# The opening layer as one program: recurrent and stick-breaking heads in 41 steps between the projections and the output product

## What is computed

```python
hn = rmsnorm(h, mix_norm[0])
qa, ka, va, qb, fb, ib, gb = split(hn @ w_in)          # seven parts of 512 columns
# stick-breaking: 8 heads of 64
z = (qa @ ka.T) / 8
log_keep = where(s < t, log_sigmoid(-z), 0)
w = where(s < t, exp(log_sigmoid(z) + later_sum(log_keep)), 0)
o_a = w @ va
# recurrent (HGRN2): 4 heads of 128, state carried from chunk to chunk
log_f = log(lb + (1 - lb) * sigmoid(fb));  k = (1 - lb) * sigmoid(-fb);  q = silu(qb)
b = cumsum(log_f)
o_b = (q exp(b)) @ state + causal(sum_k q k exp(b_t - b_s)) @ ib
o_b = rmsnorm(o_b, hg_norm) * silu(gb)
h = h + concat(o_a, o_b) @ w_out
```

## Time and profile before

| | |
|---|---|
| three runs | 3671.11, 3674.70, 3677.27 us; median 3674.7 |
| profiled execution | 3672.74 us, span 3670.9 us, mean granted clock 0.976 |
| PE busy | 3476.9 us (95%), 16522 matmuls |
| DVE, ACT, POOL busy | 1706.3 us (46%), 924.6 us (25%), 2172.9 us (59%) |
| opening layer | from 0 to 490.9 us |

### The profile page before, as it was taken

How to read it: one execution, slowest core, us unless ns; L and a number is a source line. 1 busy time by engine, 2 the same in 40 slices (tenths; PEclk the granted TensorE clock), 3 DMA queues, 4 the chain that set the end, 5 groups by cost and what they waited for, 6 DMA issues and landing times. The chain is left out here.

```text
span 3670.9 us, 46256 instructions
## 1 busy us (share of the span) xinstructions
PE 3476.9 (95%) x16522; PEld 2855.9 (78%) x16522; DVE 1706.3 (46%) x3418; ACT 924.6 (25%) x1623; POOL 2172.9 (59%) x2180
## 2 busy tenths in 40 slices
PE   7975699999879999999999999999999999999998
PEld 6754588887658888887778877788888888888887
DVE  3025554415664542424622566665555344444443
ACT  1064322202453221214531111123333311111111
POOL 5700076677316666764436767765545577878786
PEclk9987799999889999999999999999999999999999
DMA  7300022222202222222112233334444475655562
GB/s 179 110 12 0 12 98 92 104 92 98 75 24 80 98 93 103 92 98 76 59 68 92 98 132 121 138 132 181 192 184 178 180 244 195 198 198 189 184 199 98
DMA packets 134194, 439.91 MB, mean 120 GB/s; under 512 B 7131, under 2 KB 76804, under 8 KB 97156
## 3 DMA queue, kind: packets, MB, share of 16 engines
q1 hardware_dynamic: 39168, 285.23, 21.6%
q10 hardware_dynamic: 94852, 152.22, 12.3%
HBM read 362.46 MB, written 74.96 MB: 119 GB/s over the span
## 5 line engine op out<-in xcount | busy, mean ns | idle before, releaser
L192 PE MATMUL banks<-memory,weights_split 128*128 128x512 f32 x9456 | 2239.8, 395 | 31.9 <-POOL weights_split L2734 19.8
L192 PEld LDWEIGHTS banks<-memory,weights_split 128*128 128x128 f32 x9456 | 1769.5, 189 | 434.3 <-issue 59.4
L2729 POOL TENSOR_SCALAR weights_split<-weights_raw 128x512 fp32r<-128x512 f32 x1088 | 737.3, 687 | 1474.9 <-issue 838.4
L2734 POOL TENSOR_TENSOR weights_split<-weights_raw,weights_split 128x512 fp32r<-128x512 f32 x1088 | 1481.4, 1372 | 0.0
L192 PE MATMUL banks<-weights_split,memory 128*128 128x512 f32 (+1 forms) x3648 | 818.3, 386 | 0.0
L192 PEld LDWEIGHTS banks<-weights_split,memory 128*128 128x128 f32 x3648 | 678.4, 188 | 139.4 <-issue 1.0
L2491 DVE TENSOR_TENSOR memory<-memory,memory 128x512 fp32r<-128x512 f32 x128 | 168.9, 1319 | 354.4 <-ACT memory L2605 354.4
L2470 DVE TENSOR_SCALAR memory<-banks,memory 128x128 f32<-128x128 f32 x512 | 174.9, 408 | 212.6 <-PE banks L2337 204.8
L2605 ACT ACTIVATE memory<-memory 128x512 fp32r<-128x512 f32 x128 | 81.0, 634 | 600.8 <-PE banks L192 588.2
L2538 ACT ACTIVATE memory<-banks 128x512 f32<-128x512 f32 x128 | 76.7, 599 | 569.2 <-PE banks L192 569.1
L2485 DVE TENSOR_TENSOR memory<-memory,memory 128x512 f32<-128x512 f32 x128 | 164.5, 1286 | 50.8 <-DMA memory<-hidden 44.3
(11 more groups left out here) (246 smaller groups left out, 2260.0 us busy)
## 6 DMA issues: line engine op xcount, KB each, us to landing
weights_raw<-in_weights SPq DMA_DIRECT2D x272, 1024.0 KB, 4.8
hidden<-memory ACTq DMA_DIRECT2D x64, 512.0 KB, 2.6
routing<-memory ACTq DMA_DIRECT2D x16, 2048.0 KB, 6.3
memory<-routing ACTq DMA_DIRECT2D x32, 1024.0 KB, 7.9
memory<-hidden ACTq DMA_DIRECT2D x32, 1024.0 KB, 10.3
window_rows<-memory ACTq DMA_DIRECT2D x1, 3064.0 KB
chunk_rows<-memory ACTq DMA_DIRECT2D x1, 2556.0 KB
residual<-in_x ACTq DMA_DIRECT2D x4, 512.0 KB, 11.2
```

Of the source, the lines that this page charges most:

```text
L192: last = k.nc.tensor.matmul(out, left[a], right[b], start=start and n == 0, stop=stop and n == 2, skip_group_check=True)
L2729: k.nc.gpsimd.tensor_scalar(cut(high, n * PIECE, PIECE), cut(raw, n * PIECE, PIECE), 1.0, 1.0, ALU.mult, ALU.mult).then_inc(k.high_made, 1)
L2734: k.nc.gpsimd.tensor_tensor(cut(low, n * PIECE, PIECE), cut(raw, n * PIECE, PIECE), cut(high, n * PIECE, PIECE).bitcast(F32), ALU.subtract ...
```

## The change

The stages 2 to 5 become one stage with a written order (`opening_layer`) of 41 steps, t = 0 to 40.

- PE first makes 10 tiles: the four forget tiles, the four recurrent queries, and the first tile of the stick-breaking queries and keys. In the steps it makes the other projections (both value parts, then gate, query and key tiles in turn) and the first 12 of the 64 steps of the output product, `counts[t]` dense steps in step t, in three shares with the heads' products between them. The last 52 dense steps follow.
- Recurrent head i is at phase u = t - 8 i, from 0 to 13; two heads overlap. Stick-breaking head h starts at t = 9 + 4 h: scores and mask at v = 0, logarithms at v = 1, sums at v = 2, weights applied at v = 3. One head is worked at a time, 1280 columns in three groups.
- The diagonal is masked in the scores by a product with `neg_mask`, so the DVE multiplication (L925) goes. The copies of q and k (L915, L916), the gather, the turning of the stick-breaking output and all meetings in the layer go as well. Weights are applied with the values stationary, so the output comes feature-major at once (1280 columns per head in place of 10 products of 64 columns). Heads write the operand of the output product tile by tile.
- The table rows are stored later and in five DMAs: `chunk_rows` behind the four gate tiles, then `window_rows` four heads at a time between other work of ACT. ACT waits for all five to have landed (`await_written`) before step 0.
- The order of the weights in the stream follows.

The diff, cut to its core (the removed functions are printed above):

```diff
--- before.py
+++ after.py
...
-    def scalar(act):
-        act.wait_ge(built, 2)
-        act.dma_start(k.dram["chunk_rows"], chunk_rows[0:CH_HEADS, :].unsqueeze(1).broadcast_to(
-            [CH_HEADS, P, TOKENS + P - 1])).then_inc(written, 16)
-        bank.await_read(act)
-        act.dma_start(k.dram["window_rows"], rows[0:SW_HEADS, :].unsqueeze(1).broadcast_to(
-            [SW_HEADS, P, BUCKET_ROWS])).then_inc(written, 16)
-
-    def await_written(eng):
-        eng.wait_ge(written, 32)
...
+    STORES = 5
...
+    def store(self, act, n):
+        k = self.k
+        if n == 0:
+            act.wait_ge(self.built, 2)
+            act.dma_start(k.dram["chunk_rows"], self.chunk_rows[0:CH_HEADS, :].unsqueeze(1).broadcast_to(
+                [CH_HEADS, P, TOKENS + P - 1])).then_inc(self.written, 16)
+            return
+        if n == 1:
+            self.bank.await_read(act)
+        heads = slice(4 * (n - 1), 4 * n)
+        act.dma_start(k.dram["window_rows"][heads], self.rows[heads, :].unsqueeze(1).broadcast_to(
+            [4, P, BUCKET_ROWS])).then_inc(self.written, 16)
+    def await_written(self, eng):
+        eng.wait_ge(self.written, 16 * self.STORES)
...
+    LEVELS, PERIOD, STICK_AT, LAST = 7, 8, 9, 40
+    BANDS = (0, 1, 3, 2)
+    BAND_AT, BAND_SIZE = {0: 0, 1: 512, 3: 896, 2: 1024}, {j: TOKENS - P * j for j in range(BLOCKS)}
+    GROUPS = ((0, 512), (512, 512), (1024, 256))
...
+    counts = [7] * 8 + [8] + [3] * 26 + [2, 3, 3, 2, 2, 2]
...
+    def heads_at(t):
+        return [(i, t - PERIOD * i) for i in range(HG_HEADS) if 0 <= t - PERIOD * i <= 13]
+    def stick_at(t):
+        h, v = divmod(t - STICK_AT, 4)
+        return (h, v) if 0 <= h < SB_HEADS else (0, None)
...
+    def cross_uses(t):
+        for i, u in heads_at(t):
+            if u == 9:
+                yield "turn", i, 0
+            if u == 10:
+                yield "update", i, 0
+            if u == 1:
+                yield "level", i, LEVELS
+            if 2 <= u <= 8:
+                yield "level", i, u - 2
...
+    cross_banks = [Held(k, 2 + f, [free for w, free in enumerate(use_free) if w % 2 == f][-1]) for f in range(2)]
+    out_bank = Held(k, 4, (gated_up, HG_HEADS))
+    stick_banks = [Held(k, 5, (k.x_low, mixed.made_before + D_TILES))]
+    stick_banks += [Held(k, 6 + n, (weighted, 3 * SB_HEADS - 1 + n)) for n in range(2)]
+    k.next_bank = 0
...
+        def stick_scores(h):
+            rows, pair = rows_of(h), h // 2
+            if pair == 0:
+                made[9].await_read(pe)
+            else:
+                dense[3 * pair - 1].await_read(pe)
+            if h == 0:
+                for bank in stick_banks:
+                    bank.await_free(pe)
+            elif h % 2:
+                pe.wait_ge(half_low, pair + 1)
+            else:
+                pe.wait_ge(k.x_low, mixed.made_before + 2 * pair)
+            pe.wait_ge(weighted, 3 * h)
+            for j in BANDS:
+                mm(band_bank(j), keys_a[pair][rows, j * P:(j + 1) * P], queries_a[pair][rows, j * P:TOKENS],
+                   start=j != 3, stop=False, skip_group_check=True)
+                last = mm(cut(band_bank(j), 0, P), k.const("ident"), k.const("neg_mask"), start=False, stop=True,
+                          skip_group_check=True)
+                if j != 1:
+                    last.then_inc(scored, 1)
...
+        def stick_exponents(h):
+            pe.wait_ge(summed, 3 * h + 3)
+            for j in BANDS:
+                last = mm(band_bank(j), k.const("neg_tri"), band(softplus, j), start=False, stop=j == 3,
+                          skip_group_check=True)
+                for later in range(j + 1, BLOCKS):
+                    last = mm(cut(band_bank(j), (later - j) * P, BAND_SIZE[later]), k.const("neg_ones"),
+                              band(softplus, later), start=False, stop=later == BLOCKS - 1, skip_group_check=True)
+                if j != 1:
+                    last.then_inc(exponents, 1)
...
+        def stick_apply(h):
+            pe.wait_ge(weighted, 3 * h + 3)
+            if h == 0:
+                value_banks[1][BLOCKS - 1].await_read(pe)
+            for j in range(BLOCKS):
+                last = mm(stick_banks[0].memory[rows_of(h), j * P:TOKENS], cut(values_a[j], h * 64, 64), band(weights, j),
+                          start=j == 0, stop=j == BLOCKS - 1, skip_group_check=True)
+            last.then_inc(applied, 1)
...
+        opening(0)
+        normed.tensor_sums(pe)
+        opening(1)
+        rows.tensor(pe)
+        for n in range(2, 10):
+            opening(n)
+        pe.wait_ge(cleared, 6)
+        pe.wait_ge(scanned, 4 * HG_HEADS)
+        work = products()
+        def advance(count):
+            for _ in range(count):
+                next(work)
+        for t in range(LAST + 1):
+            share = counts[t] // 3
+            advance(share)
+            for use in cross_uses(t):
+                cross(*use)
+            advance(share)
+            h, v = stick_at(t)
+            if v is not None and v != 1:
+                {0: stick_scores, 2: stick_exponents, 3: stick_apply}[v](h)
+            advance(counts[t] - 2 * share)
+            for i, u in heads_at(t):
+                if u == 11:
+                    attend(i)
+                if u == 13:
+                    turn_out(i)
+        for _ in work:
+            pass
...
+        def stick_logs(h):
+            for g, (at, size) in enumerate(GROUPS):
+                act.wait_ge(exp_neg, 3 * h + g + 1)
+                a.activation(cut(part, at, size), cut(part, at, size), ACT.Ln, bias=1.0).then_inc(log1p, 1)
...
+        normed.scalar_root(act)
+        act.wait_ge(lower_made, 1)
+        a.activation(one, zero, ACT.Exp).then_inc(sigmoids, 1)
+        act.wait_ge(k.inverted, normed.ready)
+        for n in range(4):
+            gate_tile(n)
+        rows.store(act, 0)
+        for n in range(4):
+            act.wait_ge(adjusted, 2 * n + 2)
+            a.activation(forget[n], forget[n], ACT.Ln).then_inc(logged_f, 1)
+        rows.store(act, 1)
+        for n in range(4):
+            made[4 + n].await_read(act)
+            a.activation(queries_b[n], queries_b[n], ACT.Silu).then_inc(silu_q, 1)
+            if n < 3:
+                rows.store(act, 2 + n)
+        rows.await_written(act)
+        for t in range(LAST + 1):
+            active, (h, v) = heads_at(t), stick_at(t)
+            for i, u in active:
+                if 1 <= u <= LEVELS:
+                    exponent(i, u - 1)
+                if u == 8:
+                    end_exponents(i)
+                if u == 9:
+                    copy_k(i)
+            if v == 0:
+                stick_softplus(h)
+            if v == 1:
+                stick_logs(h)
+            if v == 2:
+                stick_weights(h)
+            if v == 3:
+                stick_high_part(h)
+            for i, u in active:
+                if u == 11:
+                    square(i)
+                if u == 12:
+                    root(i)
+                    silu(i)
+                if u == 13:
+                    head_high_part(i)
+            if t == 4:
+                evacuate_values(0, values_b)
+            if t == 8:
+                evacuate_values(1, values_a)
...
-    tiles = [feature(parts[n], 8) for n in (0, 1, 3, 4, 6)] + [by_token(parts[n]) for n in (2, 5)]
-    tiles += [feature(a["ab_w_out"][0], 8)]
+    qa, ka, qb, fb, gb = (feature(parts[n], 8).reshape(4, 8, P, P) for n in (0, 1, 3, 4, 6))
+    tiles = [fb, qb, qa[0:1], ka[0:1]]
+    tiles = [t.reshape(-1, P, P) for t in tiles] + [by_token(parts[n]) for n in (5, 2)]
+    for n in range(3):
+        tiles += [gb[n], qa[n + 1], ka[n + 1]]
+    out_rows = a["ab_w_out"][0].reshape(2, 4, P, D_MODEL)[::-1].transpose(1, 0, 2, 3).reshape(D_MODEL, D_MODEL)
+    first_out = feature(out_rows, 8).reshape(8, 8, P, P)
+    tiles += [gb[3], first_out[:4, 0:6].reshape(-1, P, P), first_out[:4, 6], first_out[:4, 7],
+              first_out[4:].reshape(-1, P, P)]
...
```

More of the change, by code:

```diff
@@ L1128, in tensor @@
                 for c in range(BLOCKS):
                     t = slice(c * P, (c + 1) * P)
-                    last = mm(k.banks[:, level % 2, t], k_part[level % 2][:, t], q_part[level % 2][:, t],
-                              start=True, stop=True)
-                last.then_inc(scored, 1)
-            pe.wait_ge(k_dec, i + 1)
+                    last = mm(bank[:, t], left[:, t], right[:, t], start=True, stop=True)
+                last.then_inc(crossed, 1)
+            elif kind == "turn":
+                pe.wait_ge(decayed, 2 * i + 1)
+                for c in range(BLOCKS - 1):
+                    t = slice(c * P, (c + 1) * P)
+                    last = k.nc.tensor.transpose(bank[:, t], to_end[:, t], k.const("ident"))
+                last.then_inc(turned_k, 1)
+            else:
+                pe.wait_ge(k_copied, i + 1)
+                if i == 0:
+                    value_banks[0][BLOCKS - 1].await_read(pe)
```

(48 more changed lines are left out.)

757 lines of the change are left out of this document (420 added, 337 removed).

## The result

| | before | changed |
|---|---|---|
| runs | 3671.11 to 3677.27 us, median 3674.4 (4 runs) | 3699.95 to 3704.70 us, median 3701.4 (4 runs) |
| ratio | | 1.0075, 95% interval 1.0057 to 1.0092 |
| span, mean granted clock | 3670.9 us, 0.976 | 3698.6 us, 0.971 |
| last residual addition of the opening layer starts | 490.1 us | 518.7 us |
| PE busy | 3476.9 us | 3469.7 us |

A forecast was written before the change was run, and what follows sets the result against it. PE was taken to stand waiting for the stores until 222 us; dense work 131, heads 39.5 and 78, joints 11, waits 15 and clock 8 end the layer at 505 us instead of 490.9: 3688 us, range 3650 to 3725.

The forecast's parts named there:

- Rival 1: Window stores do not queue on four engines: stores in at 137 to 140 us, kernel 3607 us; chance 0.14.
- Rival 2: Woven steps also wait 4.3 us for each of 8 heads, rows cost 0.266 us: 3749 us; chance 0.06.
- PE at level 0: Start of the opening layer: PE reaches the products of level 0 at 93 us, then stops for 129 us.
- The stores: Four window stores share four engines behind chunk_rows, issued at 50 us; all stores in at 220 us.
- ACT's issues: Before step 0: ACT's queue is busy issuing window stores until near 180 us, as each needs room in the rings.
- From the restart to the end: PE resumes at 222 us; its remaining work, waits and clock loss bring the layer's end to 505 us.
- stick-breaking heads: After the restart: 44 units of 0.222 us for scores, masks, sums and weights, 9.8 us a head, 78 us.
- Waits left: After the restart: PE waits at the sums and for the scores' bank, 15 us taken, bounds 5 and 35.
- Clock: After the restart: lowered PE clock behind one long and three short stops costs 8 us.
- Joints: After the restart: switches between dense and f32 work, 0.11 us each, some 100 of them, 11 us.
- What the weaving saves: Opening layer: some 116 us if nothing waited for the stores, ending at 375 instead of 491 us.

The follow-up runs named there:

- experiment 5: Changed kernel with one window store of 16 rows instead of four of 4, and the wait for the stores moved to before step 9; 3572.5 us.
- experiments 1 to 3: Changed kernel with window rows stored as four stores from all 16 rows, one of 16 rows, or two of 8 rows; 3615.4, 3612.5 and 3646.3 us.
- experiment 4: Changed kernel with the wait for the stores moved from before step 0 to before step 9, stores unchanged; 3660.4 us.
- Experiment 10: Experiment 7's kernel with each stick-breaking head's four scores first and then its four masks, instead of in turn; 3557.5 us.
- Experiment 7: Experiment 5's kernel with more of the output product's dense steps in the last six woven steps; 3567.0 us.
- four16: Changed kernel with four window stores, each from all 16 source rows with a quarter of their copies; 3615.4 us.
- chunk16: Experiment 7's kernel with chunk_rows stored from 16 rows, each of the 8 held twice with 64 copies; 3566.3 us.

## Why the prediction was right

The forecast was 3688 us, 14 above before; the time is 3701, 27 above. It is inside the range of 3650 to 3725, the sign is right, and the mechanism is the one that was forecast. The size is less good: the slowdown is about twice the one forecast, as the layer ends at 519.4 us and not at 505, 5.8 us of it at the restart (227.8 against 222) and 8.6 behind it. Rival 1 is excluded: the share behind `chunk_rows` is 22.6%, not 50, and the stop lasts until 227.8 us. Rival 2 too: sums wait 5.7 us over eight heads, not 4.3 in each. Point by point:

- *PE at level 0.* Forecast 93 us, found 103.7. The norm's sums come 3 us later than before (30.78 against 27.77 us), where I had them as before; weights were late once, for 5.8 us at 89 us, where I had none; and the 16 dense steps and the diagonal took 103.67 - 89.40 = 14.3 us, not 11.8, with a granted clock of 0.77 from 80 to 95 us. None of this costs anything here, since the stores set the end of the stop behind it: the stop is 124.1 us, not 129. In experiment 5, with no stop, it all lies on the path.
- *The stores.* Forecast: issued at 50, `chunk_rows` over at 107, in at 220. Found: 52.4; the share falls from about 45% to 22% near 112; 226.2. So 5 us at the start and under `chunk_rows` (0.44 us a row beside weights, 0.411 taken), 3 us in 512 window rows (0.222 on average over the 114 us, 0.217 taken), 2 us won at the signal. Four rows, four engines and the sharing of one set were right, and experiments 1 to 3 show each: 3615, 3646 and 3701 us for 16, 8 and 4 source rows of the same 3 MB.
- *ACT's issues.* Forecast to hold its queue until near 180 us, found 178.5. What I did not say is that this hold alone would stop PE: my sum has only the wait for landing in it. Both end in the same stop, but the remedy differs, as experiment 4 shows (41 us of 129). That an issue waits for room in the rings, as the prediction has it, no run shows directly; the last section has what the lengths of the issues go with.
- *From the restart to the end.* Forecast 283 us, found 518.69 + 0.69 - 227.76 = 291.6. **The mis-sized term is that of the stick-breaking heads**: 44 units of 0.222, 9.8 us a head, 78 in all. Scores and masks took 4.41 us a head instead of 14 x 0.222 = 3.11, so 10.4 us more over eight heads. I had taken the masks' price from a place where they stand beside other products on 128 rows. Experiment 10 takes 9.3 us of this away.
- *Waits left.* Forecast 15 us, found 13.7, but only 8.7 of them at the places named, sums and scores, the longest in the last two heads (2.1 us at 440 and 3.4 us at 470 us). The other 5.0 are 4.6 us at the products of a level and 0.4 at a dense matmul, which my sum did not have. Experiment 7 shows that the waits in the last heads are real cost.
- *Clock.* Forecast 8 us. The granted clock is 0.96 over 240 us and 0.94 over 53: 240 x 0.04 + 53 x 0.06 = 12.8 us, some of it idle time that costs nothing. It is 0 to 5 us more. Most of it, 40 x 0.21 = 8.4 us, lies between 440 and 480 us, around the waits of 1.6 us at 455 and 3.4 at 470 us, where the clock fell to its lower level, 1.2 GHz, and the scores and masks of the last head took 7.45 us instead of 4.4. A row of the table by stretch (columns as above, PEclk 0.50):

```profile
460.00:465.00 5.00, 5.00 (x16) 3.51 (x16) 0.00 (x0) 2.42 (x4) 0.00 (x0) 0.50 0.00 0
```

- *Joints.* The eight records of a level took 0.81 us from start to start, not the 0.89 I charged ahead of the joint; over 32 levels that is 2.6 us too much. The terms are then 10.4 - 1.3 - 2.6 and up to 4.8, together 6.5 to 11.3, against 8.6 us found; the split between clock and joints was not tested.

What the weaving saves, forecast as 116 us if nothing waited for the stores, is 99 us in experiment 5 (3671.4 - 3572.5; 12.5 of the 17 us that are missing lie in front of level 0, reached at 105.5 us and not 93), and 115 with experiments 7 and 10 added.

## What to carry to other kernels

When a DMA repeats few source rows many times, count the source rows: at 4, 8 and 16 rows they fixed how many engines it got, and cutting such a store into pieces along its rows made every piece narrower and queued the pieces on the same engines; cut along the copies instead. Before putting any wait or large store on a compute engine's queue, ask separately when it is issued, how long the issuing holds the queue, and what behind it feeds the bottleneck. Between plain f32 products, put those on 64 rows together and those on 128 rows together.

## What the runs showed of the hardware that was not expected

- A change between a product on 64 rows and one on 128 rows costs PE 0.195 us: 0.42 us for a mask beside scores (231.89 - 231.47), 0.23 beside its own kind ((229.37 - 228.46) / 4).
- How long an issue holds ACT's queue goes with the rows of earlier stores that its engines still have to do, not with its own. With `chunk_rows` on the engines from 56 to 112 us and 0.222 us a window row behind it, the four window issues of the changed kernel end when about 79, 108, 115 and 84 earlier rows are left on an engine. In `four16`, whose pieces have 32 rows on an engine and not 128, it is 79, 88, 109 and 84. In `chunk16` some 50 are left when the window store is issued, and the issue is over at once. This is worked out, not seen directly, and the mechanism stays open. The issue of the first window store in `four16`, and then that of `chunk16`:

```profile
59.53 17.98 ACTq L869 DMA_DIRECT2D window_rows<-memory  x1
```

```profile
62.26 0.56 ACTq L870 DMA_DIRECT2D window_rows<-memory  x1
```

- The rows of a store that is held like this did not start before its issue ended, though engines were free. In `four16` the window store may use all 16, but from 60 to 78 us, during its issue, the queue has less than half of them; from 78 to 92 us it has 75.7%:

```profile
q10 hardware_dynamic: 330, 0.84, 41.6%
```

- The Trainium skill ("DMA: Bandwidth & Descriptors", section "Why a DMA increments its semaphore by 16 and not by 1") has the number of engines as the largest number up to 16 that divides the slowest dimension of both sides, and places them at the lowest numbers. The runs agree with the number at 4, 8 and 16 rows: 22.6%, 45.7% and 91.7% of sixteen engines. That the stores queue on the same engines fits the placing; which engines they are, no view here shows.
- The stop of 124 us itself cost PE little by its clock: the first eight records behind it took 2.05 us instead of 1.05, and after five more microseconds the granted clock was full, 2.4 GHz:

```profile
228.00:233.00 5.00, 5.00 (x21) 4.39 (x22) 4.58 (x9) 1.26 (x2) 2.58 (x3) 0.74 0.01 3
233.00:238.00 5.00, 5.00 (x27) 4.29 (x27) 3.15 (x5) 1.38 (x2) 5.00 (x6) 1.00 0.00 0
```
